# A step planner given traced durations, a latency for each engine and TensorE's passages between array shapes

## The chip, the cores and the metric

The program runs on one core of a Trainium2 chip. The metric is the device time of one execution in microseconds (us), the median of several runs. Lower is better. TensorE is called PE in the profile, VectorE DVE, ScalarE ACT, GpSimd POOL and the sync engine, which issues all DMAs here, SP.

## The reference: three transformer blocks over 512 tokens

The model width is 1024, and everything is float32. Cut to what matters:

```python
# first block: sparse attention (8 heads, compressed keys and a window) beside a gated recurrence (4 heads)
proj = rms_norm(x, norm_mix) @ w_in
o_nsa = nsa_mixer(q, kc, vc, ks, vs, kw, vw, gates)     # softmax attention
o_hgrn = hgrn2_mixer(hq, hf, hi, hg, lb, o_gain)        # S = decay * S + k^T v, in chunks
x = x + concatenate([o_nsa, o_hgrn]) @ w_out
x = x + (silu(gate) * up) @ w_down                      # ffn 1
# second block, layer 0: differential attention; layer 1: window attention with sinks
p = softmax(where(causal, s, NEG_INF)); a = p[:, :, 0] - lam * p[:, :, 1]
x = x + (subln(a @ v)) @ w_o                            # 8 heads
x = x + swiglu(rms_norm(x), w_gate_up, w_down)          # ffn 2
x = x + swa_sink_attention(...)                         # 16 query heads, 4 key heads
x = x + swiglu(rms_norm(x), w_gate_up, w_down)          # ffn 3
```

## The kernel before

Activations are kept transposed: 8 tiles of 128 features x 512 tokens. A dense product in float32 is made of three passes over operands that are split into a high and a low part: `hi x hi`, `lo x hi`, `hi x lo` (L986, L987, L988; L960 to L962 where tokens are the output's rows). Such a triple is one step `tri`, named by its stage, its weight tile ("unit", 0 to 291, 512 KB each) and its place in it. A unit is loaded by SP (step `ld`), its high part is written by ACT (`hi`, L1289) and its low part by DVE (`lo`, L1600), two halves each; five load buffers and four high-part buffers are in rotation.

The stages in order: `in`, `vg`, `hv`, `h3` (projections of the first block), `wo` (its output), `f1` (first ffn), `dv`, `qk` (projections of differential attention), `do` (its output), `f2`, `ks`, `vs`, `sq` (window attention's projections), `so` (its output), `f3`. Attention runs between the triples: `sc` are scores (L1095; L1119 in the window attention), products with 64 contracted rows, so that they use half of the array's rows; `mx` on DVE and `ex` on ACT are the softmax; `wt` on DVE weights it; `tn` transposes on PE (L1144), `tc` copies out on ACT (L1443), `vl` is the product with the values (L1174 with "n" and L1199 with "s" fill half of the array's columns, L1186 with "d" all of it). The letter n, d or s after a step names the attention (first block, differential, window), the number the step. `qst` (L1009) is a norm's sum over a head; `lz1` and `lz4` (L996, L1001) a whole layer's, after POOL has summed the squares (`pag`, L2106). The recurrence has for each of 4 heads 7 levels of `decv` (DVE), `decg` and `dech` (POOL, L2128 and L2137), `deca` (ACT), `lmm` (PE, L1222) and `lmmv` (DVE, L2008), then `wi` and `ov` (PE). `hnd` (DVE) and `dtp` (PE, L1265) norm and transpose a head of differential attention, `omha` (ACT) and `omlv` (DVE, L1905) split it for `do`. SP also issues `swp`, which swaps halves of a tile for the rotary embedding, and `stk`, four copies of 128 KB that stack the window attention's keys.

What sets the order of all engines is a planner that runs when the program is built, and whose list PLAN is then written out engine by engine; on the chip each engine goes through its own list in order, with semaphore waits. `Order.add` takes a step with its engine, an assumed duration in ns, and what it waits for. `forwards` lays the steps down on five model clocks: the engine that is free first takes, of the steps that are ready, the one with the lowest rank (a class, then a due time, then its place). `backwards` makes due times from the end, `longest` from the longest path, and `run` repeats the two and keeps the plan that ends first in its own model. Before, everything that a step waits for is taken as ready 200 ns after its giver's end (`LAG`), on every engine, and an engine that finds nothing ready is looked at again when any engine comes free or any step ends.

## Time and profile before

| | |
|---|---|
| three runs | 1871.17, 1871.24, 1874.56 us; median 1871.24 us |
| profiled execution: its own time | 1872.81 us |
| its span, first to last instruction | 1870.7 us |
| PE / DVE / ACT / POOL busy | 99% / 60% / 42% / 15% |
| granted TensorE clock, mean | 0.999 |

The span leaves out 2.1 us around the instructions. The profiled execution took 1.6 us more than the median. A busy PE is one with a matmul in its pipeline, whose ends are modelled, so that a triple that is issued every 0.68 us leaves no gap. A row of the timeline gives the start, the duration (of the group where several are merged), and in brackets the idle time of the engine before it and what ended it.

### The profile page before, as it was taken

The numbers are of one execution on the slowest core, as the hardware profiler recorded it, in microseconds if no ns is written. First come the engines' busy times: TensorE is split into PE (matmuls) and PEld (weight loads), VectorE is DVE, ScalarE is ACT, GpSimd is POOL, SyncE is SP. The second block draws the span as 40 slices with busy tenths as digits, with TensorE's granted clock in tenths as the row PEclk, the third lists the DMA queues.
The fourth block names the chain that finished last, engine by engine and source line by source line (L and its number), as shares of the span: only waits on it lengthen the run. The fifth ranks groups of instructions, "written<-read, shape, count | busy, mean of one in ns | idle before, by whom it ended". The sixth has DMA issues, their size and how long they took to land.

```text
span 1870.7 us, 24073 instructions
## 1 busy us (share of the span) xinstructions
PE 1850.8 (99%) x9098; PEld 1481.0 (79%) x9098; DVE 1122.5 (60%) x1974; ACT 785.5 (42%) x1728; POOL 280.3 (15%) x216
## 2 busy tenths in 40 slices
PE   9999999999999999999999999999999999999999
PEld 6887777888888888776678888888877788888887
DVE  7555896744454465588875535445978765445343
ACT  6435876322232232476643323223458533233221
POOL 2000551211010121111021101101210111011010
PEclk9999999999999999999999999999999999999999
DMA  6132000333333333322133323332342233323323
GB/s 232 58 103 67 24 1 24 94 98 102 91 101 94 98 90 102 102 79 74 52 98 94 100 93 101 92 101 85 102 118 64 63 95 97 102 91 101 95 91 96
DMA packets 51538, 166.56 MB, mean 89 GB/s; under 512 B 6880, under 2 KB 7264, under 8 KB 51168
## 3 DMA queue, kind: packets, MB, share of 16 engines
q1 hardware_dynamic: 51424, 165.03, 28.8%
q8 instruction: 73, 1.20, 0.3%
q14 instruction: 41, 0.34, 0.1%
HBM read 155.04 MB, written 2.10 MB: 84 GB/s over the span
## 4 chain that ended last, share of the span: by engine, by line
PE 89%; DVE 6%; ACT 1%; DMA 1%; issue 1%; SPq 1%; POOL 0%; DVEq 0%; ACTq 0%
PE bank L986 25%; PE bank L988 24%; PE bank L987 24%; PE bank L1095 2%; PE bank L1144 2%; DVE WL L1600 2%; PE bank L960 1%; PE bank L1222 1%; PE bank L962 1%; PE bank L961 1%; PE bank L1009 1%; PE bank L1174 1%; DVE GL L1609 1%; PE bank L1186 1%; PE bank L1119 1%
## 5 line engine op out<-in xcount | busy, mean ns | idle before, releaser
L1289 ACT ACTIVATE WH<-RAW 128x512 fp32r<-128x512 f32 (+2 forms) x584 | 332.1, 612 | 773.0 <-PE bank L988 682.0
L1600 DVE TENSOR_TENSOR WL<-RAW,WH 128x512 fp32r<-128x512 f32 (+2 forms) x584 | 464.4, 830 | 80.5 <-ACT WH L1289 74.8
L986 PE MATMUL bank<-GH,WH 128*128 128x512 f32 x1088 | 433.7, 399 | 0.7 <-DVE SM L1817 0.7
L986 PE MATMUL bank<-HH,WH 128*128 128x512 f32 x1056 | 423.2, 401 | 4.6 <-DVE TMP L1709 1.7
L988 PE MATMUL bank<-GH,WL 128*128 128x512 f32 x1088 | 424.0, 390 | 0.0
L987 PE MATMUL bank<-GL,WH 128*128 128x512 f32 x1088 | 423.6, 389 | 0.0
L988 PE MATMUL bank<-HH,WL 128*128 128x512 f32 x1056 | 411.7, 390 | 0.0
L987 PE MATMUL bank<-HL,WH 128*128 128x512 f32 x1056 | 411.3, 390 | 0.0
L2156 POOL TENSOR_TENSOR TMP<-TMP,RST 128x512 f32<-128x512 f32 x66 | 116.7, 1769 | 863.9 <-DVE TMP L2071 863.9
L986 PEld LDWEIGHTS bank<-GH,WH 128*128 128x128 f32 x1088 | 204.4, 188 | 48.7 <-issue 6.8
L986 PEld LDWEIGHTS bank<-HH,WH 128*128 128x128 f32 x1056 | 198.4, 188 | 54.7 <-issue 10.2
L988 PEld LDWEIGHTS bank<-GH,WL 128*128 128x128 f32 x1088 | 204.2, 188 | 43.3
L987 PEld LDWEIGHTS bank<-GL,WH 128*128 128x128 f32 x1088 | 204.5, 188 | 42.4 <-issue 2.6
L988 PEld LDWEIGHTS bank<-HH,WL 128*128 128x128 f32 x1056 | 198.2, 188 | 42.1
L987 PEld LDWEIGHTS bank<-HL,WH 128*128 128x128 f32 x1056 | 198.5, 188 | 40.9 <-issue 2.9
L2071 DVE TENSOR_TENSOR TMP<-bank,TMP 128x512 f32<-128x512 f32 x66 | 45.6, 691 | 225.2 <-PE bank L988 225.2
L1631 DVE TENSOR_TENSOR XT<-bank,XT 128x512 f32<-128x512 f32 x96 | 66.1, 688 | 185.4 <-PE bank L988 185.3
L2068 DVE TENSOR_TENSOR TMP<-bank,RST 128x512 f32<-128x512 f32 x66 | 45.6, 691 | 107.3 <-PE bank L988 105.9
L2119 POOL TENSOR_TENSOR TMP<-TMP,RC 128x512 f32<-128x512 f32 x26 | 37.2, 1433 | 279.4 <-DVE TMP L1709 279.4
L1817 DVE CUSTOM_DVE_ANT_0 PB<-bank,CB 128x128 f32<-128x128 f32 (+3 forms) x108 | 50.0, 488 | 29.4 <-PE bank L1095 27.1
L1407 ACT ACTIVATE PB<-PB,SM 128x128 f32<-128x128 f32 (+3 forms) x108 | 59.7, 554 | 10.3 <-DVE SM L1817 10.1
L2106 POOL TENSOR_TENSOR ACC<-ACC,SQB 128x512 f32<-128x512 f32 x35 | 48.6, 1390 | 97.6 <-ACT SQB L1308 97.6
(246 smaller groups left out, 1864.6 us busy)
## 6 DMA issues: line engine op xcount, KB each, us to landing
RAW<-in_wgu SPq DMA_DIRECT2D x132, 512.0 KB, 3.5
RAW<-in_wd SPq DMA_DIRECT2D x48, 512.0 KB, 3.5
RAW<-in_wd SPq DMA_DIRECT2D x24, 384.0 KB, 3.1
RAW<-in_da_qk SPq DMA_DIRECT2D x16, 512.0 KB, 3.6
TMP<-TMP SPq DMA_DIRECT2D x104, 64.0 KB, 2.0
RAW<-in_w_inh SPq DMA_DIRECT2D x12, 512.0 KB, 3.6
RAW<-in_w_out SPq DMA_DIRECT2D x8, 512.0 KB, 3.7
RAW<-in_da_v SPq DMA_DIRECT2D x8, 512.0 KB, 3.5
```

The costliest lines, as they stand in the source:

```text
L986: e.matmul(b, w_h, hi[st.x][k], start=(k == 0), stop=False)
L987: e.matmul(b, w_h, lo[st.x][k], start=False, stop=False)
L988: done = e.matmul(b, w_l, hi[st.x][k], start=False, stop=(k == st.kt - 1))
L1289: e.activation(whs[s % NW][:, a:b], raw[s % NR][:, a:b], ACT.Copy).then_inc(S["wh"], 1)
L1407: e.activation(dst[:, 0:n], dst[:, 0:n], ACT.Exp, bias=SM[:, o:o + 1], scale=-1.0, accum_out=SM[:, o + 1:o + 2]).then_inc(S["ex"], 1)
L1600: e.tensor_tensor(wls[s % NR][:, a:b], raw[s % NR][:, a:b], whs[s % NW][:, a:b].bitcast(F), ALU.subtract).then_inc(S["wl"], 1)
L1631: e.tensor_tensor(xt[m], b, xt[m], ALU.add).then_inc(S[sem], 1)
L1817: return e.tensor_tensor_reduce(dst, src, mask, -1.0, floor, ALU.add, ALU.min, top)
L2068: e.tensor_tensor(s, b, RST[:, :], ALU.mult).then_inc(S["ff_o"], 1)
L2071: e.tensor_tensor(s, b, s, ALU.mult).then_inc(S["ff_o"], 1)
L2106: e.tensor_tensor(ACC[:, :], ACC[:, :], src, ALU.add).then_inc(S["st_acc"], 1)
L2156: e.tensor_tensor(s, s, RST[:, :], ALU.mult).then_inc(S["ff_y"], 1)
```

## The change

The planner alone is changed; no instruction is added or removed, and each engine does the same steps. What is new: the assumed durations are others; a step's readiness depends on the engine that waits (330 ns for PE, 130 for DVE, 145 for ACT, 150 for POOL, 200 for SP, 210 for ACT behind PE, none after what was there at the start); PE is charged 150, 195 or 210 ns for leaving a step on half of the array's rows or columns for a step of another shape, and 15 ns from a full one to a triple (`turn`, `shape`); and an engine with nothing to do is looked at again when one of its own steps becomes ready. One dependency is added, between triples of one output tile in two following units. The table of durations is shown in a few lines only.

```diff
-    LAG = 200
+    LAG = {"PE": 330, "ACT": 145, "DVE": 130, "POOL": 150, "SP": 200}
...
+    def lag(self, a, b):
+        if a not in self.on:
+            return 0
+        return 210 if self.on[a] == "PE" and b == "ACT" else self.LAG[b]
+    @staticmethod
+    def turn(held, step):
+        if held not in ("rows", "cols"):
+            return 15 if held == "full" and step[0] == "tri" else 0
+        if step[0] == "tri":
+            return 210
+        return 0 if shape(step) in ("rows", "cols") else 150 if step[0] in ("tn", "nst", "dtp", "c_tp", "c_k2") else 195
...
-            t = max(t, self.ends[a])
+            t = max(t, self.ends[a] + self.lag(a, engine))
...
-                free[engine] = min(later + events) if later or events else now + 1
+                free[engine] = min(soon + [now + 200])
...
+            if engine == "PE":
+                ns, held = ns + self.turn(held, step), shape(step)
...
-            self.ends[step] = now + ns + lands + self.LAG
+            self.ends[step] = now + ns + lands
...
-            before[b].append((a, lag * (at[a][2] + self.LAG)))
+            before[b].append((a, lag * (at[a][2] + self.lag(a, at[b][0]))))
...
+def shape(step):
+    if step[0] == "tri":
+        return "tri"
+    if step[0] in ("sc", "c_sc"):
+        return "rows"
+    return "cols" if step[0] == "vl" and step[1] != "d" else "full"
...
-            o.add("POOL", ("decg", h, lv), 740, ("lv1v", h), used)
-            o.add("POOL", ("dech", h, lv), 840, ("deca", h, lv), ("e_hv3", 4 + h))
-            o.add("DVE", ("lmmv", h, lv), 400, ("lmm", h, lv), kind="at")
+            o.add("POOL", ("decg", h, lv), 640, ("lv1v", h), used)
+            o.add("POOL", ("dech", h, lv), 740, ("deca", h, lv), ("e_hv3", 4 + h))
+            o.add("DVE", ("lmmv", h, lv), 354, ("lmm", h, lv), kind="at")
...
-            o.add("PE", ("vl", "n", n), w // 128 * 110 + 160, ("tc", "n", n), ("e_vgv", 3),
+            o.add("PE", ("vl", "n", n), w // 128 * 218 + 151, ("tc", "n", n), ("e_vgv", 3),
```

Where it moves instructions, three places are shown. The first is PE at the end of differential attention: scores 28, 29 and 30 of "d" (two products each, by their width 128, 256 and 384), before:

```order
L1095 MATMUL bank4<-PX 128x128
L1095 MATMUL bank5<-PX 128x128
L1095 MATMUL bank2<-PX 128x256
L1095 MATMUL bank4<-PX 128x256
L1095 MATMUL bank5<-PX 128x384
L1095 MATMUL bank2<-PX 128x384
L1144 MATMUL bank6<-CF,PB 128x128
L1265 MATMUL bank3<-CF,PX 128x128 x4
L1186 MATMUL bank7<-PX,PB 128x128
L1095 MATMUL bank4<-PX 128x512
```

And now (each line number is 27 higher: L1122 is L1095, L1013 to L1015 are L986 to L988, L1292 is L1265):

```order
L1122 MATMUL bank5<-PX 128x128
L1013 MATMUL bank1<-HH,WH 128x512
L1014 MATMUL bank1<-HL,WH 128x512
L1015 MATMUL bank1<-HH,WL 128x512
L1122 MATMUL bank2<-PX 128x256
L1122 MATMUL bank4<-PX 128x256
L1013 MATMUL bank1<-HH,WH 128x512
L1014 MATMUL bank1<-HL,WH 128x512
L1015 MATMUL bank1<-HH,WL 128x512
L1122 MATMUL bank5<-PX 128x384
L1122 MATMUL bank2<-PX 128x384
L1292 MATMUL bank3<-CF,PX 128x128 x4
```

A triple of unit 129 now stands between scores 28 and 29 and one between 29 and 30, and `dtp` 6 has moved ahead of transpose 28.

The second is PE at the end of the first block's attention, scores 62 (the two of width 512) among the last transposes, before:

```order
L1095 MATMUL bank2<-P1 128x512
L1095 MATMUL bank4<-P1 128x512
L1174 MATMUL bank7<-PB,P1 64x128 x2
L1259 MATMUL bank1<-SQB,CF 128x512
L1144 MATMUL bank6<-CF,PB 128x128 x5
L1174 MATMUL bank7<-TMP,P1 64x128 x4
```

And now:

```order
L1201 MATMUL bank7<-PB,P1 64x128 x2
L1286 MATMUL bank1<-SQB,CF 128x512
L1171 MATMUL bank6<-CF,PB 128x128 x2
L1122 MATMUL bank2<-P1 128x512
L1122 MATMUL bank4<-P1 128x512
L1171 MATMUL bank6<-CF,PB 128x128 x3
L1201 MATMUL bank7<-TMP,P1 64x128 x4
```

Transposes 59 (two blocks) and 60 (three), which followed each other, now have the scores between them.

The third is SP at the start of window attention: loads of `sq`'s weights (RAW) and the eight copies of `stk` (PX), between copies of `swp` (TMP), before:

```order
L876 DMA TMP<-TMP 32x512 x8
L887 DMA PX<-TMP 64x512 x4
L863 DMA RAW<-in_sw_q 128x1024 x2
L887 DMA PX<-TMP 64x512 x4
L863 DMA RAW<-in_sw_q 128x1024
L876 DMA TMP<-TMP 32x512 x4
```

And now:

```order
L903 DMA TMP<-TMP 32x512 x8
L914 DMA PX<-TMP 64x512 x4
L890 DMA RAW<-in_sw_q 128x1024
L914 DMA PX<-TMP 64x512 x4
L890 DMA RAW<-in_sw_q 128x1024 x2
L903 DMA TMP<-TMP 32x512 x4
```

The load of unit 212, which was the second of the pair, now stands behind the second four copies.

## Rows read from the trace of the kernel before

**Rows 1.** The page: the span, and the engines' busy time

```profile
span 1870.7 us, 24073 instructions
PE 1850.8 (99%) x9098; PEld 1481.0 (79%) x9098; DVE 1122.5 (60%) x1974; ACT 785.5 (42%) x1728; POOL 280.3 (15%) x216
```

**Rows 2.** Windows: stretch, length, busy (count) by engine, clock, DMA share, GB/s

```profile
400.00:600.00 200.00, 200.00 (x884) 165.66 (x883) 96.00 (x124) 56.62 (x99) 23.28 (x13) 1.00 0.33 98
200.00:280.00 80.00, 76.35 (x623) 58.73 (x622) 73.36 (x170) 65.17 (x170) 53.13 (x61) 1.00 0.01 2
```

**Rows 3.** Timeline of PE, 201 to 267 us: start, duration, instruction, idle before

```profile
203.02 0.41 PE L1144 MATMUL bank<-CF,PB 128*128 128x128 f32 x2 [0.61 <-ACT PB L1443]
...
204.41 0.41 PE L1144 MATMUL bank<-CF,PB 128*128 128x128 f32 x2 [0.60 <-ACT TMP L1443]
205.31 0.49 PE L1095 MATMUL bank<-P 64*128 64x128 f32 x4 [0.50 <-DVE SM L1817]
...
246.07 0.46 PE L1234 MATMUL bank<-HX 128*128 128x128 f32 x2 [0.67 <-DVE HX L2008]
...
266.17 0.49 PE L1095 MATMUL bank<-P 64*128 64x128 f32 x4 [1.13 <-DVE SM L1817]
```

**Rows 4.** Timeline of PE, the end of the first block's attention

```profile
300.52 1.13 PE L1095 MATMUL bank<-P 64*128 64x512 f32 x4
...
303.86 0.52 PE L1144 MATMUL bank<-CF,PB 128*128 128x128 f32 x3 [0.56 <-ACT TMP L1443]
...
305.48 0.52 PE L1144 MATMUL bank<-CF,PB 128*128 128x128 f32 x3 [0.52 <-ACT PB L1443]
```

**Rows 5.** Timeline of PE, the end of differential attention

```profile
925.15 0.70 PE L1095 MATMUL bank<-PX 64*128 64x256 f32 x4 [0.58 <-DVE SM L1817]
926.54 0.92 PE L1095 MATMUL bank<-PX 64*128 64x384 f32 x4 [0.69 <-DVE SM L1817]
...
929.63 2.08 PE L1095 MATMUL bank<-PX 64*128 64x512 f32 x4
```

**Rows 6.** Windows around it, the clock third from the end

```profile
925.00:930.00 5.00, 3.78 (x17) 2.41 (x19) 4.46 (x20) 3.45 (x17) 0.00 (x0) 0.82 0.00 0
930.00:940.00 10.00, 10.00 (x54) 7.43 (x53) 4.15 (x11) 5.08 (x14) 0.00 (x0) 0.92 0.00 0
```

**Rows 7.** Timeline of PE, the last head's transpose and the triple behind it

```profile
945.01 0.60 PE L1265 MATMUL bank<-CF,PX 128*128 128x128 f32 x4
...
947.17 0.50 PE L986 MATMUL bank<-HH,WH 128*128 128x512 f32 x1 [0.86 <-DVE HL L1905]
```

**Rows 8.** Timelines of SP, ACT and PE, the start of window attention

```profile
1360.36 2.17 SPq L863 DMA_DIRECT2D RAW<-in_sw_q  x2
1362.57 2.41 SPq L887 DMA_DIRECT2D PX<-TMP  x4
...
1368.93 1.15 ACT L1289 ACTIVATE WH<-RAW 128x512 fp32r<-128x512 f32 x2 [2.56 <-DMA RAW<-in_sw_q]
...
1373.75 0.47 PE L986 MATMUL bank<-HH,WH 128*128 128x512 f32 x1 [1.74 <-DVE TMP L1709]
```

**Rows 9.** Timeline of PE, the end of window attention

```profile
1465.11 1.09 PE L1199 MATMUL bank<-PX 128*64 128x128 f32 x16 [0.69 <-ACT PX L1443]
...
1467.31 0.47 PE L986 MATMUL bank<-GH,WH 128*128 128x512 f32 x1 [0.74 <-DVE SM L1817]
```

**Rows 10.** Timeline of PE, the first norm's sum

```profile
29.23 1.10 PE L996 MATMUL bank<-ACC,CF 128*128 128x512 f32 x2 [0.74 <-POOL ACC L2106]
```

**Rows 11.** Timeline of PE, from a triple to scores on half the rows

```profile
1379.29 0.39 PE L988 MATMUL bank<-HH,WL 128*128 128x512 f32 x1
1379.61 0.93 PE L1119 MATMUL bank<-PX 64*128 64x128 f32 x8
```

**Rows 12.** Groups by form, POOL's two steps of a recurrence level

```profile
L2137 POOL TENSOR_TENSOR HX<-HX,P 128x256 f32<-128x256 f32 x28 | 26.0, 935 | 7.3 <-ACT HX L1509 6.9
L2128 POOL TENSOR_TENSOR HX<-HX 128x256 f32<-128x256 f32 x24 | 18.1, 758 | 16.5 <-PE bank L1222 15.0 <-DVE HX L1980 1.2
```

More of the change, by code:

```diff
@@ L93, in add @@
         q = self.queue[engine].setdefault(kind or step[0], [])
+        self.on[step] = engine
         q.append((step, ns, after, first, lands, take, self.n))
@@ L110, in longest @@
                 left[a] = left.get(a, 0) + 1
-        length = {i[0]: i[1] + i[4] + (self.LAG if e == "PE" else 60) for e, _, i in self.items()}
+        length = {i[0]: i[1] + i[4] + (200 if e == "PE" else 60) for e, _, i in self.items()}
         tail = {s: 0 for s in needs}
@@ L145, in forwards @@
         self.ends, self.taken, self.given, self.begin, order = dict(self.end), {}, [], {}, []
-        events, unit, idle = list(self.ends.values()), 0, 0
+        unit, idle, held = 0, 0, "tri"
         while len(order) < self.n:
             engine = min(free, key=lambda e: free[e])
-            now, best = free[engine], None
+            now, best, soon = free[engine], None, []
             for q in queue[engine].values():
@@ L152, in forwards @@
                     continue
-                t, giver = self.ready(q[0])
-                if t is None or t > now:
+                t, giver = self.ready(q[0], engine)
+                if t is None:
+                    continue
+                if t > now:
+                    soon.append(t)
                     continue
@@ L162, in forwards @@
             if best is None:
-                later = [t for t in free.values() if t > now]
-                events = [t for t in events if t > now]
                 idle += 1
@@ L182, in forwards @@
             free[engine] = now + ns
-            self.ends[step] = now + ns + lands + self.LAG
-            events.append(self.ends[step])
+            self.ends[step] = now + ns + lands
         return max(free.values()), order
@@ L259, in plan @@
         for c in range(2):
-            o.add("DVE", ("lo", s, c), 620, ("hi", s, c), kind="lo", first="split")
+            o.add("DVE", ("lo", s, c), 602, ("hi", s, c), kind="lo", first="split")
     def evacuated(name, m):
@@ L357, in qk_norm @@
             free = ("sc", "s", 2 * (m - 4) + 1)
-        o.add("DVE", ("rot", *at), 1400, ("cs", *at), ("swp", *at), free)
+        o.add("DVE", ("rot", *at), 1327, ("cs", *at), ("swp", *at), free)
         if st == "ks":
@@ L364, in head_norm @@
     def head_norm(a, h, after, old=None):
-        o.add("ACT", ("hsqa", a, h), 1000, after, old, ("hn", a, h - 1) if h else None)
-        o.add("PE", ("hst", a, h), 960, ("hsqa", a, h), take=("ar" if a == "h" else "nb", ("hrsa", a, h)))
-        o.add("ACT", ("hrsa", a, h), 1250, ("hst", a, h))
-        o.add("DVE", ("hn", a, h), 1400 if a == "h" else 680, ("hrsa", a, h), a == "h" and ("e_hv3", h + 8))
+        o.add("ACT", ("hsqa", a, h), 972, after, old, ("hn", a, h - 1) if h else None)
+        o.add("PE", ("hst", a, h), 860, ("hsqa", a, h), take=("ar" if a == "h" else "nb", ("hrsa", a, h)))
+        o.add("ACT", ("hrsa", a, h), 1240, ("hst", a, h))
+        o.add("DVE", ("hn", a, h), 1392 if a == "h" else 680, ("hrsa", a, h), a == "h" and ("e_hv3", h + 8))
     def residual(name, nxt, j):
@@ L500, in plan @@
         old = ("ov", h - 2, 3) if h >= 2 else None
-        o.add("DVE", ("lv0v", h), 1500, ("e_ha", h), ("bounds2",), last[ST["h3"].u0 + 11], old)
-        o.add("ACT", ("lv0a", h), 1150, ("lv0v", h), ("table", "ln"), old)
-        o.add("DVE", ("lv1v", h), 2150, ("lv0a", h), h >= 2 and ("eqea", h - 2))
-        o.add("PE", ("base", h), 900, ("lv0v", h), ("e_hv3", 4 + h), take=("ar", ("basev", h)), kind="at")
-        o.add("DVE", ("basev", h), 700, ("base", h), kind="at")
+        o.add("DVE", ("lv0v", h), 1382, ("e_ha", h), ("bounds2",), last[ST["h3"].u0 + 11], old)
+        o.add("ACT", ("lv0a", h), 1038, ("lv0v", h), ("table", "ln"), old)
+        o.add("DVE", ("lv1v", h), 2065, ("lv0a", h), h >= 2 and ("eqea", h - 2))
+        o.add("PE", ("base", h), 893, ("lv0v", h), ("e_hv3", 4 + h), take=("ar", ("basev", h)), kind="at")
+        o.add("DVE", ("basev", h), 598, ("base", h), kind="at")
         for lv in range(7):
@@ L528, in plan @@
     for k in range(8):
[L529 to L530 removed]
+        o.add("ACT", ("mixa", k), 521, ("hn", "h", 3), ("nad", 2 * k + 1) if k < 4 else None)
+        o.add("DVE", ("mixv", k), 600, ("mixa", k))
     dense("wo")
```

174 lines of the change are left out of this document (86 added, 88 removed).

## The prediction

> **What bounds the kernel.** First the page: PE is busy for 1850.8 of 1870.7 us, and the next engine, DVE, for 60% [rows 1]. So PE is the bound nearly everywhere, and since no instruction is added or removed, the change can take away only two things: PE's 19.9 us of idle time, and what PE loses inside its busy time. Then the windows: in a stretch of the first ffn PE issues 884 passes in 200.0 us, 226 ns each, with no gap [rows 2]. A triple is 0.68 us, and such stretches, more than half of the kernel, have nothing to give. Only in 200 to 280 us is DVE nearly as full as PE: 73.4 us of 80 beside 76.4 [rows 2].
>
> Then PE's timeline, for each gap. Five are in the middle of the first block's attention and recurrence: 0.61 + 0.60 + 0.50 + 0.67 + 1.13 = 3.5 us [rows 3]. Two are at its end: 0.56 + 0.52 = 1.1 us [rows 4]. At the end of differential attention there are 0.58 + 0.69 = 1.3 us [rows 5], and 0.86 us behind the last head's transpose [rows 7]. One of 1.74 us is early in window attention [rows 8], two of 0.69 + 0.74 = 1.4 us at its end [rows 9], and one of 0.74 us before the very first norm's sum [rows 10]. That makes 10.6 us. The other 9 or so are at both ends of the program and in small gaps. A gap is counted from the modelled end of a pass, 0.39 us after its start [rows 11], while the next could begin after 0.226, so that each gap hides about 0.17 us more. There is also a loss that isn't idle: the granted clock is 0.82 of full over 925 to 930 us and 0.92 over 930 to 940 [rows 6]. At half speed (the 1.2 GHz level) these are 0.18 x 5 x 2 = 1.8 us and 0.08 x 10 x 2 = 1.6 us, so 3.4 us at half speed, which lose 1.7 us. It began after PE had stood idle twice within 2.5 us [rows 5]. Scores 31 there took 2.08 us, where four passes of the same width took 1.13 [rows 4, 5].
>
> **PE's own work.** I count the passages in both orders. From half-array steps to a triple they fall from 41 to 36, to a transposing step they rise from 40 to 50, to another full step they fall from 34 to 30. At the charges of the new table this is -5 x 0.210 + 10 x 0.150 - 4 x 0.195 = -0.3 us. The rows show the entering half: scores begin 0.32 us after the pass before them instead of 0.226 [rows 11], 0.1 us, so that charges of 0.15 to 0.21 for both halves are plausible. I take -0.3, from -1 to +1 if the kinds are priced wrongly. The Trainium skill (TensorEngine Tiling (Array Packing), Key Properties) says that changing the tiling mode drains the engine, and makes no difference between kinds. All changes of shape into or out of a half-array step number 245 before and 248 now. By that rule, at the row's 0.1 us for each, the work would grow by 0.3 us, so the passages are no source of gain by either.
>
> **The first sum of the norm.** `lz1` now comes one triple earlier. It waits for POOL, whose chain of sums doesn't move, and PE is in order: the gap of 0.74 us [rows 10] grows by that triple, +0.7 us. Nothing later there is idle enough to give it back. Between 0 and +0.7.
>
> **First block, middle.** The planner now knows 0.33 us of latency in place of 0.2, and the true length of `vl` and of the transposes, so it should fill most of the 3.5 us [rows 3]. But DVE is nearly full there, between transposes 9 and 61 of this attention PE has no triple left to fill a wait with, and one transpose (14) now stands only one step behind what it needs. I take half of it less 0.3, -1.5 us; the ends are 0 and -3.5.
>
> **First block, end.** Scores 62 now stand between transposes 59 and 60. They last 1.13 us [rows 4], more than the 0.56 of that wait: -0.6. The next wait (0.52 us) stands as it was, since nothing moved there.
>
> **Differential attention, end.** Between scores 28, 29 and 30 stand two triples of 0.68 us that came later before. They cover the gaps of 0.58 and 0.69 us: -1.3. If PE doesn't stand idle, the clock has no reason to fall: -1.7. Scores 31 come right behind `dtp` 6 and one transpose, some 0.7 us, while they need the softmax's maximum of step 30 first (0.33 + two of 0.5 us): a new wait of 0.6. Together -2.4, from -3.0 to 0 if the clock falls all the same and the wait is 1.5.
>
> **The last head's transpose.** `dtp` 7 has moved three triples ahead, and PE now has four triples of other units' work before the one that needs its result, where it had one. From 945.01 to 947.17 the chain takes 2.16 us [rows 7], the transpose 0.36 and three triples 2.04, 2.40 together: -0.9 us.
>
> **The loads of window attention.** The wait of 1.74 us at 1373.75 is for a bank that `qn` on DVE frees. That one waits behind both halves of unit 212, which wait for ACT, and ACT waited 2.56 us for a load until 1368.93 [rows 8]. PE, ACT and DVE have the same order there as before. Only SP differs: the load of unit 212 stood ahead of four copies of `stk`, and is now behind them. Their issue took 2.41 us [rows 8], so the load comes later by that: +2.4 us, all of it on the path. It would be 0 if the queue served both together anyway, and 4 if the clock fell during this wait, which would be over 4 us. The Trainium skill (DMA: Bandwidth & Descriptors, the part on HWDGE ordering) says that each DMA engine consumes descriptors in ring order, which speaks against this move. Its fabric ceiling of 435 GB/s gives an estimate of 1.2 us for the four copies' 0.5 MB, by which the sum would be 1.2 us lower than by the row of the issue.
>
> **Window attention, end.** Two triples now stand between transpose 27 and `vl` 13, and one more before the first triple that needs the last scores' banks: both gaps [rows 9] are covered, -1.4.
>
> **The rest.** About eight gaps go, with 0.17 us hidden behind each: -1.4. Of the small gaps and short late issues between 700 and 1500 us I take -0.8 (0 to -2).
>
> **Sum.** -0.3 + 0.7 - 1.5 - 0.6 - 2.4 - 0.9 + 2.4 - 1.4 - 1.4 - 0.8 = -6.2 us. The profiled execution (1872.8 us) would become 1866.6; the median stands 1.6 us below it, so 1865.0 us.
>
> **Rivals.** Changes of under 0.2% (3.7 us) can't be told from none here, so the bounds are 1867.5 and 1875.0.
>
> A, the forecast, 0.50: 1862 to 1867.5.
>
> B, the waits nearly all go, 0.22. The middle of the first block gives its whole 3.5 us (-2.0 more), the load costs nothing (-2.4), and the small gaps and the new wait go as well (-1.5): -12.1 us, 1859. For it: a planner whose charges are those of the trace sees each of these waits. Against it: DVE's 73.4 us of 80 [rows 2].
>
> C, no difference, 0.20. The middle gives nothing (+1.5) and the clock falls once, now in the lengthened wait for the load or still at 928 us (+1.7): -3.0, 1868.2.
>
> D, slower, 0.08. The recurrence's steps come later than planned. The change charges 640 and 740 ns for POOL's two steps of a level, while in the trace they took 758 and 935 [rows 12], when DVE is busy. So each of the 28 `lmm` would be placed up to 0.118 + 0.195 = 0.31 us before its operand is there, with no free triples to cover it: 28 x 0.31 = 8.7 us, and the 1.5 us of the middle aren't gained: 1875.2. It decides from 0.31 us for each. Against it: the charges before, 740 and 840, were short of the second too, and only 3.5 us of gaps came of it.
>
> **Numbers.** Likeliest 1865.0; A's own range is 1862 to 1867.5. The range over the cases is 1857.5 to 1870.5. It takes in B and C and leaves D and the far end of B out. Faster by over 0.2%: A and B, 0.72. Within it: C, 0.20. Slower: D, 0.08.
>
> **What would show it.** In the changed kernel's trace: no gaps between scores 28 and 30 of "d", and a clock of 1.00 throughout 925 to 940; no gap before transpose 60 of the first block, but one still before 61; the first `lz1` with a gap of 1.4; ACT waiting for the load of `in_sw_q` some 5 us and PE then 4. If the middle of the first block shows more than 3.5 us of gaps, D is at work. The prediction would be wrong above all by the waits in that stretch, where PE and DVE are both nearly full, so that a small shift on either makes new gaps that I can't count from this trace.

## The result: 0.33% slower, and the profile after

The changed kernel takes 1877.23 us (median of 7 runs, 1876.46 to 1880.95), the kernel before 1871.24 (7 runs, 1870.37 to 1874.56). The ratio is 1.0033, 95% interval 1.0023 to 1.0043. The forecast was 1865.0 with a range of 1857.5 to 1870.5, so sign and size were wrong. Rival D had the sign and nearly the size.

The page of the changed kernel, its first rows:

```profile
span 1875.2 us, 24067 instructions
PE 1852.5 (99%) x9098; PEld 1479.9 (79%) x9098; DVE 1118.7 (60%) x1974; ACT 783.8 (42%) x1728; POOL 279.3 (15%) x216
```

The span grew by 4.5 us, of which 2.8 are idle PE (19.9 before, 22.7 now) and 1.7 are more busy time with the same matmuls. The windows (stretch, length, busy and count by engine, clock, DMA) say where most of it is, and that the dense stretches are as they were (884 passes in 200 us):

```profile
0.00:60.00 60.00, 54.00 (x215) 40.52 (x216) 44.71 (x76) 40.79 (x70) 13.23 (x16) 1.00 0.54 190
140.00:200.00 60.00, 59.01 (x359) 41.07 (x357) 39.87 (x106) 35.54 (x92) 4.04 (x5) 1.00 0.21 67
200.00:280.00 80.00, 74.72 (x610) 57.35 (x611) 70.56 (x169) 62.61 (x162) 47.72 (x54) 0.98 0.01 2
210.00:215.00 5.00, 3.26 (x14) 1.54 (x13) 5.00 (x12) 2.78 (x7) 3.15 (x4) 0.84 0.00 0
215.00:220.00 5.00, 4.90 (x35) 3.51 (x35) 4.97 (x14) 3.83 (x11) 3.33 (x5) 0.82 0.01 3
400.00:600.00 200.00, 200.00 (x884) 165.68 (x883) 96.55 (x124) 57.66 (x100) 23.29 (x13) 1.00 0.32 98
900.00:980.00 80.00, 79.20 (x386) 60.81 (x385) 61.16 (x130) 44.67 (x120) 14.46 (x11) 1.00 0.27 83
```

Between 200 and 280 us PE idles 5.28 us, where it was 3.65 [rows 2], and for 10 us the granted clock is 0.84 and 0.82, which costs 0.16 x 5 + 0.18 x 5 = 1.7 us. That only takes the place of the clock loss at 925 to 940 us, which is gone. The additional busy time is what each gap hides: PE has 45 gaps now, where it had 32, and 13 x 0.17 = 2.2 us. PE's timeline there, the gaps of over 0.3 us:

```profile
200.52 0.63 PE L1171 MATMUL bank<-CF,PB 128*128 128x128 f32 x4 [1.51 <-ACT PB L1470]
...
212.14 0.30 PE L1171 MATMUL bank<-CF,PB 128*128 128x128 f32 x1 [1.74 <-ACT PB L1470]
...
254.27 0.52 PE L1171 MATMUL bank<-CF,PB 128*128 128x128 f32 x3 [0.41 <-ACT TMP L1470]
...
277.49 1.13 PE L1249 MATMUL bank<-HX 128*128 128x128 f32 x8 [1.00 <-DVE HX L2015]
278.95 0.63 PE L1171 MATMUL bank<-CF,PB 128*128 128x128 f32 x4 [0.33 <-ACT TMP L1470]
```

Where 0.5 and 0.6 us stood before [rows 3], two waits of 1.51 and 1.74 us stand now, both for ACT. Ahead of the first, ACT itself idled for only 0.60 us, also with `deca` waiting for `decv`, so most of that wait is ACT's own list. The next views are the timelines of DVE and of ACT ahead of the second. `deca` is L1536 now, `decv` L2025, the low part `lo` L1627:

```profile
206.57 0.42 DVE L2025 TENSOR_TENSOR HX<-HX 128x256 f32<-128x256 f32 x1
206.91 0.72 DVE L2035 COPY_PREDICATED HX<-CI,bank 128x256 f32<-128x256 uint8 x1
207.44 3.07 DVE L1627 TENSOR_TENSOR WL<-RAW,WH 128x512 fp32r<-128x512 f32 x3
210.43 0.41 DVE L2035 COPY_PREDICATED HX<-CI,bank 128x256 f32<-128x256 uint8 x1
210.76 0.41 DVE L2025 TENSOR_TENSOR HX<-HX 128x256 f32<-128x256 f32 x1
```

```profile
211.20 0.63 ACT L1536 ACTIVATE HX<-HX 128x512 f32<-128x512 f32 x1 [2.58 <-DVE HX L2025]
211.74 0.26 ACT L1470 ACTIVATE PB<-bank 128x128 f32<-128x128 f32 x1
```

The two views show one chain. Three `lo` took 3.07 us on DVE, for which the new table charges 3 x 602 ns = 1.8. `decv` stood behind them, ACT waited 2.58 us with `deca` at the head of its list, the copy `tc` (L1470) stood behind `deca`, and PE waited for `tc` at 212.14. The late engine is DVE, two lists away from the wait.

The other gaps by place. At the start the first norm's sum waits longer, and the sums behind it as well [rows 10]:

```profile
28.82 1.10 PE L1023 MATMUL bank<-ACC,CF 128*128 128x512 f32 x2 [1.03 <-POOL ACC L2133]
...
32.53 1.05 PE L1028 MATMUL bank<-CF,ACC 128*128 128x2 f32 x8 [0.54 <-DVE PB L1670]
...
38.25 1.10 PE L1036 MATMUL bank<-SQB,CF 128*128 128x512 f32 x2 [0.93 <-DVE TMP L1719]
```

At the first block's end [rows 4] one gap went and the next grew:

```profile
310.86 0.52 PE L1171 MATMUL bank<-CF,PB 128*128 128x128 f32 x3 [0.31 <-ACT PB L1470]
...
312.64 0.63 PE L1171 MATMUL bank<-CF,PB 128*128 128x128 f32 x4 [1.26 <-ACT PB L1470]
```

At the end of differential attention [rows 5 to 7] one gap of over 0.2 us is left, and the clock stays whole:

```profile
934.80 1.13 PE L1122 MATMUL bank<-PX 64*128 64x512 f32 x4 [0.24 <-DVE SM L1844]
...
947.89 0.60 PE L1292 MATMUL bank<-CF,PX 128*128 128x128 f32 x4
948.25 0.48 PE L1013 MATMUL bank<-HH,WH 128*128 128x512 f32 x1
```

```profile
925.00:930.00 5.00, 5.00 (x34) 4.16 (x34) 2.72 (x4) 1.78 (x4) 0.00 (x0) 1.00 0.12 30
930.00:940.00 10.00, 9.58 (x49) 5.87 (x50) 8.58 (x32) 7.39 (x30) 0.00 (x0) 1.00 0.00 0
```

At the start of window attention [rows 8], by the timelines of SP, ACT and PE, everything 2.74 us later than before:

```profile
1360.59 2.45 SPq L914 DMA_DIRECT2D PX<-TMP  x4
1363.08 0.58 SPq L890 DMA_DIRECT2D RAW<-in_sw_q  x1
1363.71 3.76 SPq L914 DMA_DIRECT2D PX<-TMP  x4
1367.52 1.25 SPq L890 DMA_DIRECT2D RAW<-in_sw_q  x2
```

```profile
1372.11 1.15 ACT L1316 ACTIVATE WH<-RAW 128x512 fp32r<-128x512 f32 x2 [1.77 <-DMA RAW<-in_sw_q]
```

```profile
1376.93 0.47 PE L1013 MATMUL bank<-HH,WH 128*128 128x512 f32 x1 [1.29 <-DVE TMP L1736]
```

### The profile page after: what moved, and what is told of

Its sections match the earlier page's. It is cut to its first block, busy times and chain, and to the rows that moved or that the text cites. A ratio compares the mean times of both kernels' runs of the same rounds, so it can differ in the third digit from the quotient of the medians.

```text
span 1875.2 us, 24067 instructions
## 1 busy us (share of the span) xinstructions
PE 1852.5 (99%) x9098; PEld 1479.9 (79%) x9098; DVE 1118.7 (60%) x1974; ACT 783.8 (42%) x1728; POOL 279.3 (15%) x216
## 4 chain that ended last, share of the span: by engine, by line
PE 84%; DVE 9%; issue 3%; ACT 2%; SPq 1%; DMA 1%; DVEq 0%; POOL 0%; ACTq 0%
PE bank L1013 24%; PE bank L1015 24%; PE bank L1014 24%; DVE WL L1627 2%; DVE PB L1844 1%; PE bank L987 1%; PE bank L988 1%; PE bank L989 1%; PE bank L1171 1%; PE bank L1122 1%; PE bank L1036 1%; PE bank L1213 1%; PE bank L1201 1%; DVE HX L2025 0%; ACT PB L1451 0%
## 5 line engine op out<-in xcount | busy, mean ns | idle before, releaser
L1627 DVE TENSOR_TENSOR WL<-RAW,WH 128x512 fp32r<-128x512 f32 (+2 forms) x584 | 459.9, 824 | 75.9 <-ACT WH L1316 70.1
L1013 PE MATMUL bank<-GH,WH 128*128 128x512 f32 x1088 | 433.9, 399 | 0.0
L1013 PE MATMUL bank<-HH,WH 128*128 128x512 f32 x1056 | 422.5, 400 | 3.3 <-DVE TMP L1736 1.3
L1015 PE MATMUL bank<-GH,WL 128*128 128x512 f32 x1088 | 424.0, 390 | 0.0
L1015 PE MATMUL bank<-HH,WL 128*128 128x512 f32 x1056 | 411.6, 390 | 0.0
L1013 PEld LDWEIGHTS bank<-GH,WH 128*128 128x128 f32 x1088 | 204.4, 188 | 49.7 <-issue 8.7
L1013 PEld LDWEIGHTS bank<-HH,WH 128*128 128x128 f32 x1056 | 198.5, 188 | 51.1 <-issue 8.0
L1015 PEld LDWEIGHTS bank<-GH,WL 128*128 128x128 f32 x1088 | 204.2, 188 | 42.9
L1015 PEld LDWEIGHTS bank<-HH,WL 128*128 128x128 f32 x1056 | 198.2, 188 | 41.8
L1171 PEld LDWEIGHTS bank<-CF,PB 128*128 128x128 f32 x327 | 38.0, 141 | 36.3 <-issue 20.9
L1171 PE MATMUL bank<-CF,PB 128*128 128x128 f32 x327 | 58.3, 283 | 7.9 <-ACT PB L1470 5.4
```

The costliest lines, as they stand in the source:

```text
L1013: e.matmul(b, w_h, hi[st.x][k], start=(k == 0), stop=False)
L1015: done = e.matmul(b, w_l, hi[st.x][k], start=False, stop=(k == st.kt - 1))
L1171: done = e.transpose(ptb[:, k * 128:(k + 1) * 128], src, ident)
L1627: e.tensor_tensor(wls[s % NR][:, a:b], raw[s % NR][:, a:b], whs[s % NW][:, a:b].bitcast(F), ALU.subtract).then_inc(S["wl"], 1)
```

## The experiments: eighteen kernels

The columns are from the one profiled execution of each kernel, in us: the first block (start of the span to the first triple of unit 38, the third unit of `f1`), what the clock cost in it (one minus the granted clock, summed over the stretches behind the first 60 us), PE's idle time from 200 to 280, differential attention (first triple of unit 108, in `dv`, to that of unit 138, the third of `f2`), window attention (first triple of `sq` to that of unit 226, the third of `f3`), the span. All the rest of the span is 1097.4 to 1098.2 us in every kernel, so the change acts in these three stretches alone. The ratio is to the kernel before, and rests on all executions.

| kernel | first block | its clock loss | idle 200-280 | diff. | window | span | ratio, 95% |
|---|---|---|---|---|---|---|---|
| before | 366.6 | 0 | 3.65 | 247.4 | 159.1 | 1870.7 | |
| changed | 372.5 | 1.7 | 5.28 | 244.2 | 160.9 | 1875.2 | 1.0033 [1.0023, 1.0043] |
| 1 old durations | 372.5 | 1.7 | 4.54 | 246.0 | 158.7 | 1874.9 | 1.0026 [1.0017, 1.0035] |
| 2 one latency | 373.4 | 1.7 | 7.08 | 244.5 | 158.1 | 1873.5 | 1.0016 [1.0006, 1.0025] |
| 3 no passages | 371.0 | 0 | 5.91 | 245.4 | 157.6 | 1871.4 | 1.0005 [0.9996, 1.0015] |
| 4 old waking | 378.5 | 3.4 | 9.28 | 248.6 | 157.5 | 1882.0 | 1.0059 [1.0042, 1.0075] |
| 5 before, 203 ns | 366.5 | 0 | 3.97 | 246.3 | 161.2 | 1871.6 | 0.9997 [0.9987, 1.0006] |
| 6 new durations only | 368.6 | 0 | 4.05 | 244.9 | 155.2 | 1866.2 | 0.9972 [0.9961, 0.9983] |
| 7 loaded | 364.7 | 0 | 1.00 | 244.4 | 159.8 | 1866.5 | 0.9984 [0.9975, 0.9993] |
| 8 joined lists | 368.1 | 1.7 | 3.66 | 244.2 | 158.4 | 1868.2 | 0.9986 [0.9977, 0.9995] |
| 9 changed, 327 ns | 371.7 | 1.7 | 5.10 | 246.9 | 159.7 | 1875.8 | 1.0019 [1.0009, 1.0030] |
| 10 loaded, 327 ns | 364.7 | 0 | 1.00 | 246.9 | 161.8 | 1871.0 | 0.9995 [0.9986, 1.0005] |
| 11 old rules, loaded | 368.3 | 3.4 | 1.46 | 244.7 | 154.9 | 1865.5 | 0.9964 [0.9955, 0.9974] |
| 12 best lists joined | 365.3 | 0 | 1.01 | 244.8 | 157.0 | 1864.7 | 0.9962 [0.9951, 0.9973] |
| 13 light queries | 366.9 | 0 | 2.17 | 244.3 | 160.9 | 1869.6 | 0.9997 [0.9987, 1.0006] |
| 14 loaded, DVE only | 367.2 | 0 | 3.40 | 244.6 | 162.5 | 1871.8 | 1.0002 [0.9992, 1.0012] |
| 15 loaded, POOL only | 372.5 | 3.4 | 4.89 | 245.3 | 160.1 | 1875.5 | 1.0022 [1.0013, 1.0032] |
| 16 old table, loaded | 370.0 | 1.7 | 3.22 | 245.8 | 158.9 | 1872.3 | 1.0014 [1.0005, 1.0023] |
| 17 loaded, jolted | 368.0 | 0 | 3.97 | 244.3 | 159.6 | 1870.2 | 0.9998 [0.9989, 1.0007] |
| 18 changed, jolted | 370.6 | 0 | 4.91 | 244.3 | 160.1 | 1873.3 | 1.0020 [1.0010, 1.0029] |

(Numbers 1 to 8 are the labels e1 to e8, and so on.)

A single execution carries the accident of whether the clock fell in it, and some more. Where PE had the same list in two kernels, the first block took 366.6 and 368.1 us (before and 8, which lost 1.7 to the clock), and 364.7, 364.7 and 365.3 (7, 10 and 12); window attention took 155.2 and 157.0 (6 and 12). So a difference of under 2 us between two kernels in one stretch is weak evidence, the more where the clock fell in one of them. In 7 it fell at 7.7 us, in a wait of 2.24 us for the first operands, and the first block took no longer than 10's, where it didn't fall.

The theories. **1**: the shortened durations leave the plan no slack; in the narrow form, it is the recurrence's steps on DVE and POOL, charged as if each ran alone. **2**: the shorter latencies of ACT, DVE and POOL took the slack. **3**: it is a lottery: any small change of the planner's numbers redraws the list and moves the time by as much. **4**: it is something that the new rules have in common and the durations don't matter.

### One part of the change taken back at a time (1 to 4)

1 keeps the new rules and has the table of before. 2, 3 and 4:

```diff
-        return 210 if self.on[a] == "PE" and b == "ACT" else self.LAG[b]
+        return 200
```

```diff
-                ns, held = ns + self.turn(held, step), shape(step)
+                held = shape(step)
```

```diff
-                free[engine] = min(soon + [now + 200])
+                later = [t for t in free.values() if t > now]
+                events = [t for t in events if t > now]
+                free[engine] = min(later + events) if later or events else now + 1
```

> The changed planner with the durations of before; latencies by engine, passages, waking and the new dependency stay. Theory 1 (the shortened durations of DVE, ACT and POOL leave no slack in the first block, where DVE and POOL slow each other down): the 4.7 us that the first block's attention lost come back, so 1871 to 1873 us, and PE's gaps between 190 and 290 us sum to 4 us or less, where the changed kernel has about 7. Theory 2 (the latencies of 130 to 150 ns in place of 200 took the slack): this stays at 1877 or worse. Theory 3 (any change of the numbers reshuffles the list, and where the waits fall is accident): anywhere between 1868 and 1881, with new waits at other places.

> The changed planner with 200 ns of latency behind every step, as before, whichever engine waits; durations, passages and waking stay new. Theory 1: no better than the changed kernel, 1876 to 1879. Theory 2: 1870 to 1872, and the first block loses no more than before. Theory 3: 1868 to 1881, at random.

> The changed planner without the charge for leaving half-array steps. Theories 1 and 2: PE's plan runs ahead of the chip by 23 us over the whole program (163 charges), so PE comes late and its operands are ready: fewer gaps than the changed kernel, 1872 to 1875, without the cause being the passages as such. Theory 3: 1868 to 1881, at random.

> The changed planner, but an idle engine is looked at again when any engine comes free or any step ends, which with latencies by engine isn't when its own step becomes ready. An idle engine may thus take a step later than it could, in the plan alone. Theory 1: 1876 to 1880, since the durations are as short. Theory 3: 1868 to 1881, at random.

None brings the first block back to 366.6 us: 372.5, 373.4, 371.0 and 378.5. So theory 1 in its broad form and theory 2 don't hold alone. The new waking is worth 6.0 us there (4.3 without the clock's part), not a cost; 4, with a median of 1884.3 us, came out slower than every theory had it. Charging the passages costs the first block nothing: the 1.5 us to 3 are no more than the clock's 1.7. Over the whole kernel 3 is 0.28% faster than the changed one, most of it in window attention (160.9 to 157.6).

### A jolt, the durations alone, the load charged, and joined lists (5 to 8)

5 is the kernel before with `LAG = 203`. 6 has before's planner with the new table. 7 is the changed kernel with the recurrence's steps charged by what they took in the trace when both engines worked:

```diff
-            o.add("DVE", ("decv", h, lv), 328, ("lv1v", h), used)
-            o.add("POOL", ("decg", h, lv), 640, ("lv1v", h), used)
+            o.add("DVE", ("decv", h, lv), 530, ("lv1v", h), used)
+            o.add("POOL", ("decg", h, lv), 700, ("lv1v", h), used)
```

and likewise `dech` 740 to 870, `lmmv` 354 to 450, the scan's step 2065 to 2240, and `wh0v`, `wh2v`, `eqmg` 1885, 1242, 1230 to 2300, 1700, 1300. 8 writes the lists of before, except from the first ffn to the middle of the second, where it writes those of the changed kernel.

> The planner of before with its one latency at 203 ns in place of 200, nothing else: a number that no one would expect to matter. Theory 3 (sensitivity: which waits fall where is accident, and the plan of before was a good draw in the first block): the first block, up to the first ffn, takes 2 to 8 us more than in the kernel before, 1873 to 1879 in all. Rival theory 4 (something that all new plans share costs the first block its 4.4 to 12 us): no difference by stage of over 1 us, 1870 to 1873.

> The planner of before (one latency of 200, no passages, its own waking) with the new durations and the new dependency. Theory 3: first block 2 to 8 us more, in all 1872 to 1880. Theory 4 with the durations as the shared cause is already weakened by the run with the old ones, which lost 6.1 us in the first block too; with rules as the shared cause: no loss here in the first block, 1868 to 1872.

> The changed planner with the recurrence's steps on DVE and POOL charged as the trace shows them under load (a level's decv 530, lmmv 450, decg 700, dech 870 ns, the scan's step 2240, wh0v 2300, wh2v 1700, eqmg 1300). Theory 1 in its narrow form (charges of an unloaded DVE and POOL make the first block late): the first block loses under 2 us against the kernel before, where the changed kernel lost 6.0; 1870 to 1873. Theory 3: again 2 to 8 us more there, unrelated.

> The two plans joined in the middle of the first and of the second ffn, where all engines have done the same steps: before's order for the first block, the changed one for differential attention, before's for window attention. If the losses are where the two traces put them, each stage keeps its time: 0, -3.2 and 0 us, a span of 1867.5 and some 1868 to 1869.5 us, ratio 0.998. If what one stage wins is lost behind it: no faster than before.

5 met neither case. Its first block stayed (366.5 us), against theory 3, but window attention took 2.1 us more and differential attention 1.1 less, against theory 4; the total can't be told from before's. 6 is faster than both kernels, 0.9972. So the new table isn't the fault by itself: with the old rules it costs the first block 2.0 us and gives 2.5 and 3.9 us later. 7 takes the first block from 372.5 to 364.7 us. Its window, beside the one of the changed kernel above:

```profile
200.00:280.00 80.00, 79.00 (x667) 61.46 (x667) 71.93 (x179) 65.38 (x173) 49.13 (x58) 1.00 0.01 2
```

8 shows that the stretches add up: its differential attention takes the changed kernel's 244.2 us within before's lists. Its first block took 1.5 us more than before with the same list, by the clock (last section).

### Is it the load or the draw? (9 to 12)

9 and 10 are the changed kernel and kernel 7 with `"PE": 327` for 330. 11 has before's rules with 7's table, 12 joins 7's lists, up to the middle of the second ffn, to 6's.

> The changed planner with the latency to TensorE charged at 327 ns instead of 330, which says nothing new of the chip but moves 265 neighbouring pairs of TensorE's list and 205 of VectorE's, about as many as the run with the loaded charges moved (198 and 149). It is the placebo beside that run. If the narrow form of theory 1 holds (the unloaded charges of VectorE and GpSimd in the recurrence cost the first block its 6 us), the first block stays long: 370 us or more from the program's start to triple 38 of the last dense stage ahead of the sequence, and the ratio to before is 1.001 or more. If theory 3 holds (any jolt of the list redraws the lot), the first block has an even chance to come back to 367 us or under.

> The kernel with the recurrence charged as under load (0.9984 of before when measured) with the same 3 ns jolt to its latency. Narrow theory 1: the first block stays within 2 us of that kernel's 364.7 us, ratio 0.997 to 1.001. Theory 3: its gain was a draw, and the first block may stand anywhere from 363 to 373 us; over 369 us speaks for it.

> Before's rules (one latency of 200 ns, no charge for passages, old waking) with the changed table of durations, and in it the recurrence charged as under load. With the changed table alone these rules gave 0.9972. Narrow theory 1: charging the load is worth something here too, but less, since the rules kept slack: first block 364 to 368 us, against 367.8 us (70.3 + 69.0 + 229.3, less nothing) of that kernel, which is 368.6. Theory 3: no relation, 363 to 373 us. A rival in between (theory 4: only the changed rules, which put recurrence steps to TensorE late in no slack, need the load charged): no difference beyond 1 us.

> The best stages together: up to the middle of the second feed-forward network the list of the kernel with the loaded recurrence (364.7 us for the first block, 244.4 us for the differential attention), behind it the list of before's rules with the changed durations (155.2 us for the window attention). If stages add up, as the graft before showed within 2 us: 364.7 + 371.8 + 244.4 + 348.2 + 26.1 + 155.2 + 351.5 = 1861.9 us of span, a median 1.5 to 3 us above it, 0.994 to 0.996 of before. If a stage's time hangs on how the stage ahead of it ended, one of the last three terms is off by over 2 us.

The placebo 9 stays long, as the narrow form wants. 10 turned out to have the same list as 7 for PE in the first block, so it repeats 7's time there (364.7) and tests nothing in it. In the later stretches its 3 ns cost 2.5 and 2.0 us, which is the lottery of theory 3. 11 cuts the idle time of 6 from 4.05 to 1.46 us, but its first block is only 0.3 us shorter, because the clock fell at its end. That cost 0.5 x 5 = 2.5 us in the window shown and 3.4 in all, so without it the block would be 3.7 us shorter than 6's. By the ratios 11 can't be told from 6:

```profile
305.00:310.00 5.00, 4.34 (x21) 3.31 (x22) 2.08 (x3) 2.64 (x5) 0.00 (x0) 0.50 0.00 0
```

12 was to take 1861.9 us by its parts and took 1864.7, since window attention took 157.0 us and not 155.2. It can't be told from 11, and both are faster than the kernel before and the changed one.

### The mechanism by itself (13), and which engine (14 to 16)

13 leaves the changed kernel's lists as they are and leaves out three quarters of the product that `dech` makes on POOL. It is a probe, and no kernel to be used:

```diff
-                e.tensor_tensor(v[:, :, m:2 * m], v[:, :, m:2 * m], q3[:, :, m:2 * m],
+                n = 64 // m
+                e.tensor_tensor(v[:, :n, m:2 * m], v[:, :n, m:2 * m], q3[:, :n, m:2 * m],
```

14 has only the DVE numbers of 7, 15 only the POOL ones, 16 is kernel 1 with 7's numbers for the recurrence.

> The changed kernel, its lists untouched, but GpSimd's multiplication of the decayed keys by the queries (the step dech, 28 times) is done on the first 128 columns of 512 alone; the other three quarters of the product are left out. If GpSimd's work stretches VectorE's steps beside it and delays what waits for dech, as the narrow form of theory 1 has it, the decay steps of VectorE (614 ns each between 190 and 280 us, charged 328) fall towards 450 ns, and the idle PE between 200 and 280 us falls from 5.3 us to 1 to 3 us; ratio to before 1.000 to 1.002. If VectorE's steps are long for another reason, their mean stays within 5% and only the waits for dech go: idle 4 to 5 us, ratio 1.002 to 1.0035.

> The changed planner with only VectorE's recurrence steps charged as under load (2240 for the scan's step, 530 for decv, 450 for lmmv, 2300 and 1700 for the last two); GpSimd's stay at 640, 740 and 1230. If VectorE's undercharged steps did the harm: idle PE from 200 to 280 us is 1 to 2 us, the first block 364 to 367 us, ratio 0.998 to 1.000. If it was GpSimd's: 5 us of idle and 370 to 373 us, ratio 1.001 to 1.004.

> The other half: only GpSimd's recurrence steps charged as under load (700, 870, 1300). Mirror image: if VectorE's charges did the harm, idle from 200 to 280 us stays at 4 to 6 us and the first block at 370 us or more, ratio 1.001 to 1.004; if GpSimd's, 1 to 2 us, 364 to 367 us, ratio 0.998 to 1.000. Both may help in part, since their deficits are 28 times 0.3 and 28 times 0.19 us.

> The changed rules with before's table of durations (1.0026 when measured, 372.6 us for the first block, 4.5 us of idle PE from 200 to 280 us), and in it only the recurrence charged as under load. If the recurrence's charges are the whole of the first block's loss under the changed rules, whatever the rest of the table says: idle 1 to 2 us and a first block of 364 to 368 us, ratio 0.998 to 1.000. If before's table cost the block something of its own under these rules, the idle stays above 3 us.

13 is the direct test, and it gives 5.6 us in the first block (372.5 to 366.9) with no step moved. Of these, 1.7 are the clock, which did not fall here. All its ten executions have a shorter span (1868.8 to 1871.6 us) than any of the changed kernel's seven (1874.3 to 1878.9). `dech` fell from 902 to 414 ns. Groups of DVE by form between 190 and 280 us, of the changed kernel and then of 13 (busy, mean ns):

```profile
L2025 DVE TENSOR_TENSOR HX<-HX 128x256 f32<-128x256 f32 x26 | 15.7, 614 | 0.6 <-PE bank L1249 0.6
L1627 DVE TENSOR_TENSOR WL<-RAW,WH 128x512 fp32r<-128x512 f32 x4 | 4.6, 1180 | 0.0
L2010 DVE TENSOR_TENSOR HX<-HX 128x512 f32<-128x512 f32 x4 | 3.9, 971 | 0.4
L1923 DVE TENSOR_TENSOR P<-bank,P 128x512 f32<-128x512 f32 x5 | 3.4, 687 | 2.6 <-PE bank L1201 2.6
L2015 DVE TENSOR_TENSOR HX<-bank,CF 128x512 f32<-128x512 f32 x4 | 2.7, 682 | 0.0
```

```profile
L2025 DVE TENSOR_TENSOR HX<-HX 128x256 f32<-128x256 f32 x27 | 14.6, 549 | 0.6 <-PE bank L1249 0.6
L1627 DVE TENSOR_TENSOR WL<-RAW,WH 128x512 fp32r<-128x512 f32 x4 | 4.0, 1034 | 0.0
L1923 DVE TENSOR_TENSOR P<-bank,P 128x512 f32<-128x512 f32 x5 | 3.4, 685 | 2.8 <-PE bank L1201 2.8
L2010 DVE TENSOR_TENSOR HX<-HX 128x512 f32<-128x512 f32 x4 | 3.2, 804 | 0.4
L2015 DVE TENSOR_TENSOR HX<-bank,CF 128x512 f32<-128x512 f32 x4 | 2.7, 682 | 0.0
```

With less work on POOL, the steps with both operands in SBUF became 11 to 17% shorter, and those with one in a PSUM bank kept their 685 and 682 ns. The Trainium skill (SBUF — State Buffer, Who interferes with whom) says that a `tensor_tensor` of VectorE with both inputs in SBUF contends with GpSimd's reads for a shared port; the trace agrees, by the 11 to 17% above. The decay steps fell to 549 ns, not to the 450 that I expected. The idle time fell from 5.28 to 2.17 us, as expected. The wait at 212 in the changed kernel is here 0.89 us, at 210.52, behind three `lo` that took 2.48 us:

```profile
206.41 2.48 DVE L1627 TENSOR_TENSOR WL<-RAW,WH 128x512 fp32r<-128x512 f32 x3
```

How much of the 5.6 us came from the shorter `dech` itself and how much from DVE beside it, this run can't separate. The mean length of `decv` alone doesn't decide: in kernel 9 it was 536 ns, and PE idled 5.10 us all the same. Nor was it new. Before's own groups in the same stretch, `decv` and `lo`:

```profile
L1998 DVE TENSOR_TENSOR HX<-HX 128x256 f32<-128x256 f32 x27 | 15.9, 601 | 1.4 <-PE bank L1222 1.4
L1600 DVE TENSOR_TENSOR WL<-RAW,WH 128x512 fp32r<-128x512 f32 x4 | 3.0, 779 | 0.0
```

So the decay steps were as long before, and far over their charge of 370 ns then; `lo` took less. The change lowered that charge to 328 and the latencies from 200 to 130 to 150, and with them the slack. That this is why waits grew is argued from 7 to 18, and no run shows it by itself. Before's lists with the lighter `dech` were not run, so it isn't shown how much of 13's gain the changed lists alone account for.

14 came out between its two cases (367.2 us, 3.40 of idle), and 15 as its case against POOL's charges had it (372.5, 4.89). But 15's trace lost 3.4 us to the clock and the changed kernel's 1.7. With that taken off, the first block is 3.6 us shorter by DVE's charges, 1.7 by POOL's and 6.1 by both. The ratios, 1.0033 for the changed kernel, then 1.0002, 1.0022 and 0.9984, say the same, though 15 can't be told from the changed kernel by them. 16 gained 2.5 us, and kept 3.22 us of idle where I expected 1 to 2: before's table costs these rules something outside the recurrence too.

### One lucky list? (17 and 18)

Both have `"DVE": 127` for 130, once with the loaded charges and once without.

> The changed planner with the recurrence charged as under load, and the latency to VectorE at 127 ns instead of 130. Of TensorE's 540 steps in the first block 158 have another neighbour than in the run with the loaded charges (364.7 us, 1.0 us of idle from 200 to 280 us). If the charges are the cause: first block 364 to 368 us and idle of 0.5 to 2.5 us. If that run was one lucky list: 369 to 374 us and idle of 4 to 7 us, as in the lists without the charges. What the later stages make of it is a draw of some 2 us each.

> Its partner without the charges: the changed kernel with the same 127 ns. If the charges are the cause: first block 370 to 374 us, idle from 200 to 280 us of 4 to 7 us, ratio 1.001 to 1.004. If the lists are a lottery, it may come down to 367 us.

17 came out between the two cases that it was to tell apart: 368.0 us is within the first, 3.97 us of idle is outside both. Five pairs, without and with the load charged, now stand in the first block: 372.5 and 364.7 (7), 372.5 and 370.0 (1 and 16), 368.6 and 368.3 (6 and 11), 370.6 and 368.0 (18 and 17), and 371.7 and 364.7 (9 and 10, the same list as 7). The loaded one is never longer, has less idle time in each, and the lower ratio. Outside of 7's list it gains 0.3 to 2.6 us, or 2.5 to 3.7 with the clock's part taken off. With 7's list it gains 7.8 and 7.0, or 6.1 and 5.3. So by these pairs the charge is worth some 2.5 to 3.7 us in the first block, and the rest of 7's gain is probably that list's luck.

## Why the prediction was wrong, point by point

**The middle of the first block (forecast -1.5).** This is the step that failed, with the sentence "I take half of it less 0.3". The measured first block is +5.9 us: 1.8 of idle time at the start, 2.5 between 60 and 400 us (1.0 of it between 140 and 200, where there was none), and a rest of 1.6. The clock alone cost 1.7, and seven more gaps at 0.17 would hide 1.2, so that some 1.3 us came back in a way that wasn't taken apart. In the stretch that the forecast was about, 200 to 280 us, PE idles 1.6 us more and the clock costs 1.7, where 1.5 were to be gained. The row against it stood in the text: DVE busy 73.4 of 80 us. I let the planner's new numbers speak, though [rows 12] showed that POOL's steps take longer than the old charges, and the change shortened them. I also didn't look at how long `decv` and `lo` take when POOL works: 601 and 779 ns before, in a trace that I had, and 614 and 1180 now, against the 328 and 602 that the new table charges. Charging the load gave some 2.5 to 3.7 us back (7 to 18), and taking work off POOL 5.6, with the clock (13).

**Rival D (0.08).** Its place, its sign (1875.2, the profiled span now is 1875.2 and the median 1877.23) and its test, over 3.5 us of gaps in the middle, came true. Its working did not: `lmm` is not late 28 times by 0.31 us. Two waits of 1.5 and 1.7 us appear where ACT's list has `deca` ahead of a copy, and one of 1.0 for DVE itself, and DVE, not POOL alone, is what is late. What I held against it, that the old charges were short as well and only 3.5 us came of it, is answered by the pairs 1 and 16: those charges cost 2.5 us under the new rules. That 1875.2 is nearly what was measured is luck: its 8.7 us are for waits that the trace doesn't show, and the span's 4.5 are the sum of +5.9 in the first block, -3.2 in differential and +1.8 in window attention. The chance was far too low.

**The first norm's sum (+0.7).** The gap itself grew by 0.29 us, to 1.03. But two sums behind it now wait 0.54 and 0.93 us, the second of which waited 0.20 before, and in the first 60 us PE idles 6.00 us where it idled 4.25. "Nothing later there is idle enough to give it back" was right, and what is queued behind it was missed.

**The first block's end (-0.6).** The scores cover the first gap, as forecast. The wait went to the last transpose but one (1.26 us), so that the sum of all gaps there (1.57 us, where the first block's end had 0.56 + 0.52 and a third of 0.67) fell by 0.2.

**Differential attention and the last head (-2.4 and -0.9).** Right in mechanism: no gap between scores 28 and 30, none behind the last transpose, and a clock of 1.00. From 900 to 980 us idle PE fell from 3.25 to 0.80 us, and the clock rose from 0.98 to 1.00 (1.6 us). The new wait for scores 31 is 0.24, not 0.6. But 0.6 us of new idle time between 700 and 900 took some of it back, and the stretch as a whole gained 3.2 us.

**The load behind `stk` (+2.4).** Mis-sized: +0.44. Counted from the same triple, the load of unit 212 was issued 3.8 us later (at 1367.52 for 1360.98, less 2.74), but it landed 4.6 us after its issue, where it took 7.9 before, beside the copies that followed it. ACT waited for it until 1372.11, which is 1368.93 + 2.74 + 0.44. ACT's wait was 1.77 us and PE's 1.29, and not some 5 and 4. Its issue before, by the timeline of SP:

```profile
1360.98 1.54 SPq L863 DMA_DIRECT2D RAW<-in_sw_q  x1
```

The lower end of that term, the queue serving both together, was the right one. The row of the issue is the time that SP is busy, not what a load behind it loses.

**Window attention's end (-1.4).** Both gaps went, but smaller ones came, five of them of 0.18 to 0.63 us: 14 in the stretch instead of 5. Their idle time is only 0.4 us more, but the stretch is 1.8 us longer, as nine more gaps that hide 0.17 each would have it (1.5). With before's rules the same table takes 155 us here. Each of the new rules taken back gives 2.8 to 3.4 us in it (2 to 4). Which waits these are was not taken apart.

**PE's own work (-0.3).** Busy time rose by 1.7 us. The clock's loss moved but stayed 1.7, and 13 more gaps hide 2.2, which leaves -0.5 for the passages: within the bounds taken.

**What stays open.** The new rules lengthen the first block with either table: 366.6 to 372.5 us with the old one, 368.6 to 372.5 with the new (4.2 and 2.2 us without the clock's 1.7), and 370.6 and 370.0 with 3 ns less in one latency (18, and 9 without the clock's part). No single rule accounts for it. With the recurrence charged as under load, 0 to 3.4 us of it are left: 364.7, 368.0 and 368.3 us with the new rules (7, 17, 16), and 364.9 with the old (11), each without the clock's part. Lists made with 3 ns more or less in one latency differ by 0.1 to 3.3 us in this stretch (5, 9, 18, and 17 beside 7), so a part of the loss can't be told from the draw. The added dependency between triples was never taken back alone. It is in every new list with a longer first block, but in 7 too, whose first block is the shortest, and what it costs isn't known.

## What to carry to other kernels

A planner's table should hold what a step takes where it runs: here a decay step of DVE took 614 ns beside a POOL that was busy for 47.7 of 80 us, 549 beside one with less work, and was charged 328. Such a charge plans the steps too close. Where an in-order list is planned that tightly, look two engines back from a forecast wait, and ask what the row ahead of it on each list would have to take.

Before a gain or loss of 0.3% from a planner's change is believed, jolt one of its numbers by 1 or 2% and time that as well: here such jolts alone moved a stretch by up to 3.3 us and the whole kernel by up to some 2.6 (ratio 0.9984 to 0.9998 from 7 to 17), and the same list in another execution moved a stretch by up to 1.8. And if the stretches of a list can be joined, choose for each the plan that measured best there.

## What the runs showed of the hardware that was not expected

The granted clock can fall in one execution of a list and stay whole in another. Kernel 8 has before's lists up to the first ffn. The window of 8 and then of before:

```profile
305.00:310.00 5.00, 3.82 (x21) 2.88 (x22) 3.53 (x7) 4.32 (x9) 0.00 (x0) 0.68 0.00 0
```

```profile
305.00:310.00 5.00, 3.85 (x30) 3.03 (x31) 3.70 (x7) 4.71 (x10) 0.00 (x0) 1.00 0.00 0
```

PE's timeline of 8, and of before, at the same transpose behind the same gap:

```profile
306.70 1.01 PE L1741 MATMUL bank<-CF,PB 128*128 128x128 f32 x4 [0.67 <-ACT PB L2040]
```

```profile
306.67 0.63 PE L1144 MATMUL bank<-CF,PB 128*128 128x128 f32 x4 [0.67 <-ACT PB L1443]
```

The gaps ahead of it are 0.57 and 0.51 us in 8 and 0.56 and 0.52 in before, and 8's next transpose began at 310.40 us, where before's began at 308.83, 1.5 us of it lost behind this one. In kernel 15 the clock stood at 0.50, the 1.2 GHz level, after gaps of 0.39, 1.50 and 0.34 us within 3.3 us, and four passes of scores took 2.08 us. So a wait on PE can cost more than its length, and whether it does can't be read from one trace.
